# Halves of tokens for the second layer's input, and its first two score blocks inside the first gate projection

## The chip, the cores and the metric

The kernel runs on one core of one Trainium2 chip. The metric is the device time of one execution in microseconds; less is better. The kernel uses five engines: TensorE (PE; its weight loads are listed as PEld), VectorE (DVE), ScalarE (ACT), GpSimd (POOL) and SyncE (SP), which here only issues DMAs.

## The reference

Two layers over 1024 tokens of width 1024, and a final norm. Layer 0 is a gated delta rule with 8 heads; layer 1 is causal stick-breaking attention with 8 heads of 128.

```python
def stick_breaking_branch(h, w_in, w_out):
    q, k, v, gate = jnp.split(h @ w_in, 4, axis=-1)      # 8 heads of 128 each
    ...
        z = jnp.einsum('bhqd,bhsd->bhqs', q_blk, k).astype(jnp.float32) * scale
        log_1m = jnp.where(mask, jax.nn.log_sigmoid(-z), 0.0)
        tail = lax.cumsum(log_1m, axis=3, reverse=True) - log_1m
        A = jnp.where(mask, jnp.exp(jax.nn.log_sigmoid(z) + tail), 0.0)
        return jnp.einsum('bhqs,bhsd->bhqd', A.astype(v.dtype), v)
    ...
    return (o * jax.nn.silu(gate)) @ w_out

def reference(...):
    h = h + gated_deltanet_branch(rmsnorm(h, norm_w[0]), ...)
    h = h + stick_breaking_branch(rmsnorm(h, norm_w[1]), ...)
    return rmsnorm(h, final_norm_w)
```

## The kernel before

**Layout.** The residual `xT` is kept with its 1024 channels on the partitions, as eight blocks `cb` of 128 channels by 1024 tokens (five in `home`, three in `late`). A projection of one block of 128 outputs is 48 matmuls over 512 tokens: 8 blocks of channels, two halves of tokens, and three parts, because each float32 product is made as w_hi·u_hi + w_hi·u_lo + w_lo·u_hi. The weights are split by ScalarE (`split_hi`, w_hi) and GpSimd (`split_lo`, w_lo). The input is split by ScalarE (`u_upper`: u_hi = xT times the norm weight, rounded) and VectorE (`u_lower`: u_lo, what is left of it). The norm's factor per token is applied later, to the products.

**Groups and banks.** Every 24 matmuls over one half of the tokens form a group. Groups are numbered through the whole kernel and take PSUM banks 0 and 1 in turn; `proj_ready` counts those that TensorE has finished, `proj_taken` those that ScalarE or VectorE has read. TensorE starts a group only when the one two before it has been taken. `("b", h, b)` is a projection of head h in the second layer: b = 0 is q, 1 is k, 2 the gate, 3 is v.

**End of the first layer.** The output projection's last 16 groups (`last_group`, 6 matmuls each) run as i = 0 to 15, with half = i // 8 and cb = i % 8: first all blocks for the first 512 tokens, then all for the second. VectorE adds each group to `xT` (`add_output`, line 1197). After the add of a second-half group, ScalarE does `u_upper(1, cb)` over all 1024 tokens (line 789) and `square(1, cb)` (line 783), GpSimd adds the squares (`add_squares`, line 637), VectorE does `u_lower(1, cb)` over all 1024 tokens (line 1079), and only then its next add. square(cb) waits for the sum two blocks back. ScalarE's and GpSimd's streams also hold the splits of the first weights of layer 1 there, before block 4 and at the end.

**Start of the second layer.** TensorE runs ("b", 0, 0) block by block as u_lo comes, with `block_sum(1)` (line 1517: the sum of the squares over the channels) after 36 of its 48 matmuls, then ("b", 0, 1), then `rms_to_tokens(1)` (line 1525), then the gate ("b", 0, 2) and v ("b", 0, 3). ScalarE makes the norm's factor out of block_sum (lines 794, 796) and then takes each group (`take_b`, line 806). Then come a meeting of all engines (`all_arrived(…, 2)`), needed because the attention's buffers lie where others lay, and the scores.

**Attention.** Each head has eight blocks of queries, longest first. For a block, TensorE makes the scores into banks 2 and 3 or 4 and 5 (`scores`, line 1739), VectorE masks the diagonal (`mask`, line 1409), ScalarE takes Abs, Exp and Ln (`softplus`, lines 1020 to 1024), VectorE adds (`softplus_sum`, 1414), scans (`scan`, 1421) and subtracts (`exponent`, 1428, counted by `arg_done`), and ScalarE takes Exp (1031). `scores(h, s + 2)` waits for the exponent of block s, whose banks it takes. Between these, `attend` gives TensorE the matmuls of the next head's four projections, in numbers written out by hand (`STEP_FILL`). On VectorE q and k are scaled by `scale_qk` (lines 1395 and 1397, counted by `bqk_done`). For head 0 VectorE's stream is scale_qk, mask(0, 0), softplus_sum(0, 0), mask(0, 1), scan(0, 0), exponent(0, 0), and then `attend`, which begins with softplus_sum(0, 1), mask(0, 2), scan(0, 1).

Every engine runs its instructions in the order written; a wait holds up all that stands behind it on that engine. The end of the kernel is the output projection and the final norm.

Of the kernel before, what the change touches and what calls it, by code (L numbers as in the profile page):

```python
# [22 lines left out]
ALU = mybir.AluOpType  # L23
ACT = mybir.ActivationFunctionType
F32 = mybir.dt.float32
# [5 lines left out]
KB = D // P  # L31
NC = T // P
H = 8
HALF = 512
MMS = 3 * KB
# [46 lines left out]
def build(nc, x, norm_w, a_w_in, a_conv_w, a_a_log, a_dt_bias, a_o_norm, a_w_out,  # L82
          b_w_in, b_w_out, final_norm_w, out):
    V, A, G, PE = nc.vector, nc.scalar, nc.gpsimd, nc.tensor
# [10 lines left out]
    with ExitStack() as ctx:  # L95
# [8 lines left out]
        u_hi = sb("u_hi", [P, KB, T], F32R)  # L104
# [3 lines left out]
        u_lo = sb("u_lo", [P, KB, T], F32R)  # L108
# [8 lines left out]
        cols = sb("cols", [P, P])  # L117
# [4 lines left out]
        NORM_COL, ONORM_COL = 96, 120  # L122
# [5 lines left out]
        def xT(cb):  # L128

            return home[:, cb, :] if cb < HOME else late[:, cb - HOME, :]  # L130
# [102 lines left out]
        proj_ready, proj_taken = sem("proj_ready"), sem("proj_taken")  # L233
        u_hi_done, u_lo_done = sem("u_hi_done"), sem("u_lo_done")
# [11 lines left out]
        rst_ready, rst_done = sem("rst_ready"), sem("rst_done")  # L246
# [96 lines left out]
        FIRST, FREED = {}, {}  # L343
# [6 lines left out]
        LAST_GROUP = FIRST["last", 0]  # L350
# [37 lines left out]
        U_ROUND = {"gate": 0, ("b", 0, 0): 1, ("out", 0): 2}  # L388
        BY_K = ("gate", ("z", H - 1), ("early", 0), ("b", 0, 0), ("out", 0))

        def products(key, first, last):

            n, by_k, ks = NUMBER[key], key in BY_K, heads_of(key)
            for m in range(first, last):
                if by_k:
                    k, half, part = m // 6, m % 6 // 3, m % 3
                else:
                    half, k, part = m // (3 * ks), m % (3 * ks) // 3, m % 3
                if m == 0:
                    PE.wait_ge(lo_done, n + 1)  # L400
                if k == 0 and part == 0 and n > 0:

                    PE.wait_ge(proj_taken, FIRST[key] + half - 1)
                if key in U_ROUND and half == 0 and part == 0:
                    PE.wait_ge(u_lo_done, KB * U_ROUND[key] + k + 1)
                if key == ("early", 0) and half == 0 and part == 0:
                    PE.wait_ge(oe_lo, k + 1)
                mm = PE.matmul(psum[:, half], (w_hi, w_hi, w_lo)[part][:, n % 2, k],  # L408
                               (u_hi, u_lo, u_hi)[part][:, k, half * HALF:(half + 1) * HALF],
                               start=k == 0 and part == 0, stop=k == ks - 1 and part == 2)  # L410
                if k == ks - 1 and part == 2:
                    mm.then_inc(proj_ready, 1)
                elif key == ("z", H - 1) and half == 1 and part == 2:
                    mm.then_inc(u_free, 1)
# [62 lines left out]
        def half_range(half):  # L477

            return slice(half * HALF, (half + 1) * HALF)
# [299 lines left out]
        def _(act):  # L779
            def square(rnd, cb):  # L780
                if cb >= 3:
                    acc_done.wait(act, rnd, cb - 2)
                A.activation(acc[:, :] if cb == 0 else sq[:, cb % 2], xT(cb), ACT.Square
                             ).then_inc(sq_done.handle, 1)

            def u_upper(rnd, cb):

                col = NORM_COL + KB * rnd + cb
                A.activation(u_hi[:, cb, :], xT(cb), ACT.Copy, scale=cols[:, col:col + 1]
                             ).then_inc(u_hi_done, 1)  # L790
# [194 lines left out]
            norm_scale(H - 1, 1)  # L985
            late_hi(H - 1, 1)

            for cb in range(KB):
                if cb == KB // 2:
                    split_hi(("b", 0, 0))  # L990
                act.wait_ge(proj_taken, LAST_GROUP + KB + cb + 1)
                if cb == EARLY:
                    act.wait_ge(proj_ready, FREED["last", 1])
                u_upper(1, cb)
                square(1, cb)
            split_hi(("b", 0, 1))
            inverse_rms(1)
            arrive(act)
# [12 lines left out]
                if half == 1:  # L1011
                    split_hi(after_next(("b", nh, b)))

            for e in range(7):
                take_b(0, e)

            def softplus(h, s):
                w, slot, bk = (Q_BLOCKS[s] + 1) * P, s % 2, 2 + 2 * (s % 2)
                mask_done.wait(act, h, s + 1)
                A.activation(soft[:, slot, 0:w], banks(bk)[:, 0:w], ACT.Abs).then_inc(soft_a.handle, 1)  # L1020
                soft_a.wait(act, h, s + 1)
                A.activation(soft[:, slot, 0:w], soft[:, slot, 0:w], ACT.Exp, scale=-1.0).then_inc(soft_b.handle, 1)
                soft_b.wait(act, h, s + 1)
                A.activation(soft[:, slot, 0:w], soft[:, slot, 0:w], ACT.Ln, bias=1.0).then_inc(soft_c.handle, 1)
# [21 lines left out]
                    fill.to(STEP_AT[4 * s + 2])  # L1046
                fill.to(QUAD - MMS)

            for s in range(2):
                softplus(0, s)  # L1050
            for h in range(H - 1):
                attend(h, True)
            attend(H - 1, False)
# [21 lines left out]
        def _(dve):  # L1075
            def u_lower(rnd, cb):
                col = NORM_COL + KB * rnd + cb
                dve.wait_ge(u_hi_done, KB * rnd + cb + 1)
                V.scalar_tensor_tensor(out=u_lo[:, cb, :], in0=xT(cb), scalar=cols[:, col:col + 1],  # L1079
                                       in1=u_hi[:, cb, :].bitcast(F32), op0=ALU.mult, op1=ALU.subtract  # L1080
                                       ).then_inc(u_lo_done, 1)

            def output_lower(rnd, k):

                dve.wait_ge(u_hi_done, KB * rnd + k + 1)
                V.tensor_tensor(u_lo[:, k, :], o_all[:, k, :], u_hi[:, k, :].bitcast(F32),
                                ALU.subtract).then_inc(u_lo_done, 1)
# [30 lines left out]
            def by_head(t):  # L1118
# [18 lines left out]
                                   op0=ALU.max, op1=ALU.add).then_inc(gate_dve, 1)  # L1137
            dve.wait_ge(gate_dve, 4)
            V.scalar_tensor_tensor(out=graw[:, :, :], in0=by_head(gtmp[:, 3]), scalar=-1.0,
                                   in1=row_a[:, 2, :].unsqueeze(2).broadcast_to((P, H, NC)),  # L1140
                                   op0=ALU.mult, op1=ALU.mult).then_inc(gate_dve, 1)
# [6 lines left out]
                                   in0=gtmp[:, 0].rearrange("p n h -> p (n h)").rearrange("p (h n) -> p h n", h=H),  # L1148
                                   scalar=-1.0, in1=gates[:, :, 0, :],
                                   op0=ALU.mult, op1=ALU.mult).then_inc(gate_dve, 1)  # L1150
# [233 lines left out]
            late_lo(H - 1, 1, 4)  # L1384
            for i in range(2, 2 * KB):
                add_output(i % KB, LAST_GROUP + i, 16 * (KB - HOME))
                if i >= KB:
                    u_lower(1, i % KB)
            arrive(dve)
            rms_by_tokens(1)  # L1390
            all_arrived(dve, 2)
# [55 lines left out]
            def attend(h, follow):  # L1447
                for s in range(NC):
                    ahead = (h, s + 1) if s + 1 < NC else (h + 1, 0)
                    there = follow or s + 1 < NC  # L1450
                    if there:
                        softplus_sum(*ahead)
                    if s + 2 < NC:
                        mask(h, s + 2)
                    elif follow:
                        mask(h + 1, s + 2 - NC)
                    if there:
                        scan(*ahead)
                    copy_aT(h, s, 0)
                    if s == 0:  # L1460
                        scale_v(h, 0)
                    if there:
                        exponent(*ahead)
                    copy_aT(h, s, 1)
                    if s == 0:
                        scale_v(h, 1)
                    if s == 4:
                        gate_out(h, 0)
                    if s == 5 and follow:
                        scale_qk(h + 1)  # L1470
                    if not follow and s < H - 1:
                        output_lower(2, s)
                gate_out(h, 1)

            dve.sem_inc(bo_done.handle, 2)
# [18 lines left out]
                V.tensor_tensor(xT(cb)[:, half_range(half)], psum[:, half], xT(cb)[:, half_range(half)], ALU.add  # L1494
                                ).then_inc(proj_taken, 1)

            output_lower(2, H - 1)
            for cb in range(KB):
                for half in range(2):
                    add_block(cb, half)  # L1500
# [1 line left out]
            for n in range(NC):  # L1502
                dve.wait_ge(fin_rs, n + 1)
                if n >= 4:
                    dve.wait_ge(out_done[n % 4], 16 * (n // 4))
                V.scalar_tensor_tensor(out=fin_o[:, n % 4], in0=banks(FIN_BANKS[n % 4]), scalar=fin_s[:, n, 1:2],
                                       in1=fin_w[:, :], op0=ALU.mult, op1=ALU.mult).then_inc(fin_done, 1)
# [3 lines left out]
        def _(pe):  # L1511
# [210 lines left out]
            products(("b", 0, 0), 36, 2 * MMS)  # L1722
            products(("b", 0, 1), 0, 2 * MMS)
            rms_to_tokens(1)
            for b in range(2, 4):
                products(("b", 0, b), 0, 2 * MMS)

            def project(h, first, last):

# [5 lines left out]
            def scores(h, s):  # L1735
                w, bk, qb = (Q_BLOCKS[s] + 1) * P, 2 + 2 * (s % 2), Q_BLOCKS[s]
                for c in range(0, w, HALF):
                    n = min(HALF, w - c)
                    mm = PE.matmul(psum[:, bk + c // HALF, 0:n], b_q[:, qb * P:(qb + 1) * P],  # L1739
                                   b_k[:, c:c + n], start=True, stop=True)  # L1740
                mm.then_inc(sc_ready.handle, 1)
# [67 lines left out]

            all_arrived(pe, 2)  # L1810
            bqk_done.wait(pe, 0, 2)
            for s in range(2):
                scores(0, s)
            for h in range(H - 1):
                attend(h, True)
            attend(H - 1, False)
# [36 lines left out]
```

## Time and profile before

| | us |
|---|---|
| Median of 3 runs (1483.81 to 1485.61) | 1483.94 |
| The profiled execution | 1485.75 |
| Its span in the trace | 1484.0 |
| TensorE matmul busy | 1389.5 (94%) |
| VectorE busy | 894.7 (60%) |
| ScalarE busy | 638.0 (43%) |
| GpSimd busy | 433.8 (29%) |

The profile is one execution. Times in the rows are microseconds from the start of its span, and 1.75 us of the profiled execution lie around the span. The busy share of TensorE counts pipelined matmuls and is no measure of its speed; its clock is given as the share of full speed that was granted, 1.00 for 2.4 GHz and 0.50 for 1.2 GHz. In a timeline, a bracket holds how long the engine was idle ahead of the row and which operation ended that.

### The profile page before, as it was taken

The numbers are of one execution on the slowest core, as the hardware profiler recorded it, in microseconds if no ns is written. First come the engines' busy times: TensorE is split into PE (matmuls) and PEld (weight loads), VectorE is DVE, ScalarE is ACT, GpSimd is POOL, SyncE is SP. The second block draws the span as 40 slices with busy tenths as digits, with TensorE's granted clock in tenths as the row PEclk, the third lists the DMA queues.
The fourth block names the chain that finished last, engine by engine and source line by source line (L and its number), as shares of the span: only waits on it lengthen the run. The fifth ranks groups of instructions, "written<-read, shape, count | busy, mean of one in ns | idle before, by whom it ended". The sixth has DMA issues, their size and how long they took to land.

```text
span 1484.0 us, 18475 instructions
## 1 busy us (share of the span) xinstructions
PE 1389.5 (94%) x7351; PEld 1137.4 (77%) x7351; DVE 894.7 (60%) x1532; ACT 638.0 (43%) x879; POOL 433.8 (29%) x230
## 2 busy tenths in 40 slices
PE   5898999999999999988996989999999999998897
PEld 4687787888888888877884768778787877876785
DVE  7387777869697878776336145564546455557313
ACT  6153435253535353542325235544454445546113
POOL 6443334334233333434125311221122122211120
PEclk9999999999999999998999989999999999999999
DMA  7211110101111111030211200111111111000302
GB/s 188 55 29 29 29 36 22 51 22 37 36 36 29 36 36 36 23 120 12 75 43 57 57 29 29 29 44 29 29 29 43 29 29 29 29 30 0 114 29 114
DMA packets 97190, 65.20 MB, mean 44 GB/s; under 512 B 2401, under 2 KB 91602, under 8 KB 97106
## 3 DMA queue, kind: packets, MB, share of 16 engines
q1 hardware_dynamic: 97106, 64.04, 14.5%
q8 instruction: 58, 0.95, 0.3%
q14 instruction: 26, 0.21, 0.0%
HBM read 53.54 MB, written 10.49 MB: 43 GB/s over the span
## 4 chain that ended last, share of the span: by engine, by line
PE 80%; DVE 12%; ACT 3%; issue 2%; POOL 1%; DMA 0%; POOLq 0%; SPq 0%; DVEq 0%; PEldq 0%; ACTq 0%
PE psum L408 51%; PE psum L1739 4%; PE psum L1765 4%; DVE terms L1299 3%; PE psum L1752 2%; PE psum L1681 2%; PE psum L1626 2%; PE psum L1696 2%; PE psum L1651 2%; PE psum L1672 2%; DVE stick L1421 1%; PE psum L1635 1%; DVE small_L L1284 1%; PE psum L1577 1%; DVE Xs L1292 1%
## 5 line engine op out<-in xcount | busy, mean ns | idle before, releaser
L408 PE MATMUL psum<-u_hi,w_hi 128*128 128x512 f32 x1264 | 523.9, 414 | 27.7 <-DVE u_lo L1079 7.6
L408 PE MATMUL psum<-u_lo,w_hi 128*128 128x512 f32 x1264 | 517.5, 409 | 0.0
L408 PE MATMUL psum<-u_hi,w_lo 128*128 128x512 f32 x1264 | 506.8, 401 | 0.0
L381 POOL TENSOR_TENSOR w_lo<-w_raw,w_hi 128x1024 fp32r<-128x1024 f32 (+1 forms) x83 | 211.9, 2554 | 716.8 <-ACT w_hi L376 716.8
L408 PEld LDWEIGHTS psum<-u_hi,w_hi 128*128 128x128 f32 x1264 | 240.8, 190 | 82.8 <-issue 21.7
L408 PEld LDWEIGHTS psum<-u_lo,w_hi 128*128 128x128 f32 x1264 | 240.8, 190 | 50.5 <-issue 7.2
L408 PEld LDWEIGHTS psum<-u_hi,w_lo 128*128 128x128 f32 x1264 | 240.4, 190 | 49.7 <-issue 3.8
L376 ACT ACTIVATE w_hi<-w_raw 128x1024 fp32r<-128x1024 f32 (+1 forms) x83 | 85.8, 1034 | 159.0 <-PE psum L408 114.3
L708 POOL TENSOR_TENSOR Lb<-dec,level 128x512 f32<-128x512 f32 (+1 forms) x64 | 89.0, 1406 | 126.2 <-PE psum L1681 68.9
L1168 DVE SCALAR_TENSOR_TENSOR late<-raw,cols,late 128x1024 f32<-128x1024 f32 x72 | 120.1, 1668 | 1.9
L1020 ACT ACTIVATE soft<-psum 128x1024 f32<-128x1024 f32 (+3 forms) x64 | 41.7, 652 | 162.1 <-DVE psum L1409 161.5
L1409 DVE TENSOR_TENSOR psum<-psum,causal 128x128 f32<-128x128 f32 x64 | 19.0, 297 | 143.7 <-PE psum L1739 143.7
L915 ACT ACTIVATE v_new<-psum 128x128 f32<-128x128 f32 x64 | 17.7, 277 | 188.5 <-PE psum L1597 188.5
L1421 DVE TENSOR_TENSOR_SCAN stick<-soft 128x1024 f32<-128x1024 f32 (+3 forms) x64 | 97.7, 1526 | 0.0
L1436 DVE COPY aT<-psum 128x512 f32<-128x512 f32 (+1 forms) x96 | 52.3, 545 | 69.3 <-PE psum L1752 69.3
L1739 PE MATMUL psum<-b_k,b_q 128*128 128x512 f32 (+1 forms) x192 | 76.4, 509 | 15.3 <-DVE stick L1428 14.9
L1765 PEld LDWEIGHTS psum<-aT,b_v 128*128 128x128 f32 x576 | 75.0, 195 | 4.5
L1189 DVE TENSOR_TENSOR raw<-psum,rsb 128x512 f32<-128x512 f32 x64 | 43.8, 687 | 56.5 <-PE psum L408 56.5
L1299 DVE TENSOR_TENSOR terms<-Xs,small_T 128x16 f32<-128x16 f32 (+14 forms) x120 | 71.5, 596 | 9.7 <-DVE small_T L1304 0.5
L806 ACT ACTIVATE b_raw<-psum 128x512 f32<-128x512 f32 x64 | 38.0, 593 | 91.2 <-PE psum L408 91.1
L1765 PE MATMUL psum<-aT,b_v 128*128 128x128 f32 x576 | 76.0, 278 | 0.0
L1739 PEld LDWEIGHTS psum<-b_k,b_q 128*128 128x128 f32 x192 | 35.7, 194 | 41.5 <-DVE stick L1428 17.9
(208 smaller groups left out, 2022.2 us busy)
## 6 DMA issues: line engine op xcount, KB each, us to landing
w_raw<-in_a_w_in SPq DMA_DIRECT2D x33, 512.0 KB, 4.1
w_raw<-in_b_w_in SPq DMA_DIRECT2D x32, 512.0 KB, 4.0
x_stage<-in_x SPq DMA_DIRECT2D x8, 512.0 KB, 7.4
w_raw<-in_b_w_out SPq DMA_DIRECT2D x8, 512.0 KB, 3.6
out<-fin_o SPq DMA_DIRECT2D x8, 512.0 KB, 2.6
resid<-late SPq DMA_DIRECT2D x6, 512.0 KB, 2.6
o_rows<-o_nrm SPq DMA_DIRECT2D x12, 256.0 KB, 2.0
w_raw<-in_a_w_out SPq DMA_DIRECT2D x8, 384.0 KB, 3.2
```

The costliest lines, as they stand in the source:

```text
L376: A.activation(tiles(w_hi, key), tiles(w_raw, key), ACT.Copy).then_inc(hi_done, 1)
L381: G.tensor_tensor(tiles(w_lo, key), tiles(w_raw, key), tiles(w_hi, key).bitcast(F32), ALU.subtract).then_inc(lo_done, 1)
L408: mm = PE.matmul(psum[:, half], (w_hi, w_hi, w_lo)[part][:, n % 2, k], (u_hi, u_lo, u_hi)[part][:, k, half * HALF:(half + 1) * HALF], star ...
L708: G.tensor_tensor(Lb[:, g, :, used], half_of(dec, g)[:, :, used], level[:, l:l + 1, used].broadcast_to((P, 4, used.stop)), ALU.mult).then_ ...
L1020: A.activation(soft[:, slot, 0:w], banks(bk)[:, 0:w], ACT.Abs).then_inc(soft_a.handle, 1)
L1168: V.scalar_tensor_tensor(out=conv[:, s], in0=tap, scalar=by, in1=conv[:, s], op0=ALU.mult, op1=ALU.add).then_inc(convs.handle, 1)
L1189: V.tensor_tensor(raw[:, slot, 3 + half * HALF:3 + (half + 1) * HALF], psum[:, half], rsb[:, half_range(half)], ALU.mult).then_inc(proj_ta ...
L1299: V.tensor_tensor(terms[:, :, 0:r + 1], row_L[:, r % 2, :, 0:r + 1], small_T[:, :, 0:r + 1], ALU.mult).then_inc(terms_done.handle, 1)
L1421: V.tensor_tensor_scan(stick[:, slot, 0:w][:, ::-1], soft[:, slot, 0:w][:, ::-1], soft[:, slot, 0:w][:, ::-1], 0.0, ALU.add, ALU.bypass).t ...
L1436: V.tensor_copy(aT[:, s % 2, 4 * g:4 * g + n], bank(6, n)).then_inc(at_done.handle, 1)
L1739: mm = PE.matmul(psum[:, bk + c // HALF, 0:n], b_q[:, qb * P:(qb + 1) * P], b_k[:, c:c + n], start=True, stop=True)
L1765: mm = PE.matmul(psum[:, 7, t], b_v[:, blk, :], aT[:, s % 2, blk], start=blk == 0, stop=blk == qb)
```

## The change

The input of the second layer is made in halves of 512 tokens: the first halves of u_hi and u_lo of a block follow its first-half group, the second halves its second-half group. VectorE does each half of u_lo one add later than its block's own add (in the first sweep two adds later). The squares stay whole. As there are now sixteen counts of u_lo_done for this layer, the later waits count from 3·KB.

In TensorE's stream, the meeting of the engines, the wait for q and k, and scores(0, 0) move to the middle of the gate's projection, and scores(0, 1) to its end, ahead of v's projection. ScalarE's stream is changed to match: softplus(0, 0) ahead of the take of the gate's second half, softplus(0, 1) ahead of that of v's first half. VectorE's stream of the attention stays as it was.

```diff
@@ products
-                    PE.wait_ge(u_lo_done, KB * U_ROUND[key] + k + 1)
+                    PE.wait_ge(u_lo_done, (0, 2 * KB, 3 * KB)[U_ROUND[key]] + k + 1)
@@ scalar
+            def u_upper_half(cb, half):
+
+                col = NORM_COL + KB + cb
+                A.activation(u_hi[:, cb, half_range(half)], xT(cb)[:, half_range(half)], ACT.Copy,
+                             scale=cols[:, col:col + 1]).then_inc(u_hi_done, 1)
...
-            for cb in range(KB):
-                if cb == KB // 2:
+            for i in range(2 * KB):
+                half, cb = i // KB, i % KB
+                if i == KB + KB // 2:
                     split_hi(("b", 0, 0))
-                act.wait_ge(proj_taken, LAST_GROUP + KB + cb + 1)
+                act.wait_ge(proj_taken, LAST_GROUP + i + 1)
                 if cb == EARLY:
-                    act.wait_ge(proj_ready, FREED["last", 1])
-                u_upper(1, cb)
-                square(1, cb)
+                    act.wait_ge(proj_ready, LAST_GROUP + KB * (half + 1))
+                u_upper_half(cb, half)
+                if half == 1:
+                    square(1, cb)
             split_hi(("b", 0, 1))
...
-            for e in range(7):
+            for e in range(5):
                 take_b(0, e)
...
-            for s in range(2):
-                softplus(0, s)
+            softplus(0, 0)
+            take_b(0, 5)
+            softplus(0, 1)
+            take_b(0, 6)
             for h in range(H - 1):
                 attend(h, True)
@@ vector
+            def u_lower_half(cb, half):
+                col = NORM_COL + KB + cb
+                dve.wait_ge(u_hi_done, KB + half * KB + cb + 1)
+                V.scalar_tensor_tensor(out=u_lo[:, cb, half_range(half)], in0=xT(cb)[:, half_range(half)],
+                                       scalar=cols[:, col:col + 1], in1=u_hi[:, cb, half_range(half)].bitcast(F32),
+                                       op0=ALU.mult, op1=ALU.subtract).then_inc(u_lo_done, 1)
...
             for i in range(2, 2 * KB):
                 add_output(i % KB, LAST_GROUP + i, 16 * (KB - HOME))
-                if i >= KB:
-                    u_lower(1, i % KB)
+                if i < KB:
+                    u_lower_half(i - 2, 0)
+                elif i == KB:
+                    for cb in range(KB - 2, KB):
+                        u_lower_half(cb, 0)
+                if i > KB:
+                    u_lower_half(i % KB - 1, 1)
+            u_lower_half(KB - 1, 1)
             arrive(dve)
...
-                        output_lower(2, s)
+                        output_lower(3, s)
...
-            output_lower(2, H - 1)
+            output_lower(3, H - 1)
@@ tensor
             rms_to_tokens(1)
-            for b in range(2, 4):
-                products(("b", 0, b), 0, 2 * MMS)
+            products(("b", 0, 2), 0, MMS)
...
             all_arrived(pe, 2)
             bqk_done.wait(pe, 0, 2)
-            for s in range(2):
-                scores(0, s)
+            scores(0, 0)
+            products(("b", 0, 2), MMS, 2 * MMS)
+            pe.wait_ge(rst_done, 2)
+            scores(0, 1)
+            products(("b", 0, 3), 0, 2 * MMS)
```

## Rows read from the trace of the kernel before

**Rows 1.** The page: the chain's shares by engine, and a DMA issue.

```profile
PE 80%; DVE 12%; ACT 3%; issue 2%; POOL 1%; DMA 0%; POOLq 0%; SPq 0%; DVEq 0%; PEldq 0%; ACTq 0%
w_raw<-in_b_w_in SPq DMA_DIRECT2D x32, 512.0 KB, 4.0
```

**Rows 2.** The chain that ended last, 770 to 885: start, us, what.

```profile
782.50 7.06 PE psum L425 x30
...
805.81 0.69 DVE late L1197
...
809.14 0.69 DVE late L1197
...
813.18 9.16 PE psum L408 x33
...
827.32 11.17 PE psum L408 x48
...
840.17 21.88 PE psum L408 x96
...
864.13 1.03 ACT soft L1020
...
866.28 1.06 ACT soft L1024
```

**Rows 3.** Windows: stretch, us, busy time (count) of five engines, granted clock, DMA.

```profile
790.00:806.00 16.00, 8.78 (x34) 5.73 (x33) 9.89 (x11) 11.44 (x11) 9.30 (x4) 1.00 0.01 1
...
813.18:815.91 2.73, 2.73 (x6) 2.16 (x7) 1.49 (x1) 2.26 (x3) 2.59 (x2) 0.50 0.48 192
813.18:822.18 9.00, 9.00 (x33) 7.33 (x34) 1.49 (x1) 3.15 (x3) 8.71 (x4) 0.84 0.36 117
...
872.30:878.24 5.94, 5.94 (x17) 4.20 (x18) 3.92 (x3) 4.96 (x6) 2.37 (x1) 0.56 0.01 3
```

**Rows 4.** Timeline of GpSimd: start, us, line, operation, output and inputs, shapes, [idle before].

```profile
795.58 2.54 POOL L637 TENSOR_TENSOR acc<-acc,sq 128x1024 f32<-128x1024 f32 x1 [17.21 <-ACT sq L783]
...
802.02 2.78 POOL L637 TENSOR_TENSOR acc<-acc,sq 128x1024 f32<-128x1024 f32 x1 [0.55 <-ACT sq L783]
804.77 3.37 POOL L381 TENSOR_TENSOR w_lo<-w_raw,w_hi 128x1024 fp32r<-128x1024 f32 x1
808.09 12.54 POOL L637 TENSOR_TENSOR acc<-acc,sq 128x1024 f32<-128x1024 f32 x4
```

**Rows 5.** Timeline of VectorE, 770 to 885.

```profile
781.10 0.69 DVE L1208 TENSOR_TENSOR u_lo<-o_raw,u_hi 128x512 fp32r<-128x512 f32 x1 [0.70 <-ACT u_hi L904]
...
804.38 1.51 DVE L1079 SCALAR_TENSOR_TENSOR u_lo<-home,cols,u_hi 128x1024 fp32r<-128x1024 f32 x1 [1.22 <-ACT u_hi L789]
...
840.43 3.19 DVE L1395 SCALAR_TENSOR_TENSOR b_q<-b_raw,rsb 128x1024 f32<-128x1024 f32 x1
843.55 1.21 DVE L1397 TENSOR_TENSOR b_k<-b_raw,rsb 128x1024 f32<-128x1024 f32 x1
```

**Rows 6.** Timeline of ScalarE, 770 to 885.

```profile
780.44 0.63 ACT L904 ACTIVATE u_hi<-o_raw 128x512 fp32r<-128x512 f32 x1 [3.31 <-DVE o_raw L1232]
...
791.36 1.04 ACT L783 ACTIVATE acc<-home 128x1024 f32<-128x1024 f32 x1
...
825.25 1.06 ACT L796 ACTIVATE rsb<-rsb 128x1024 f32<-128x1024 f32 x1
```

**Rows 7.** Timeline of TensorE, line 1739; the last row is of the chain.

```profile
861.88 3.38 PE L1739 MATMUL psum<-b_k,b_q 128*128 128x512 f32 x8
872.30 2.93 PE L1739 MATMUL psum<-b_k,b_q 128*128 128x512 f32 x4 [7.03 <-DVE stick L1428]
...
924.28 1.99 PE L1739 MATMUL psum<-b_k,b_q 128*128 128x512 f32 x4
...
941.36 1.45 PE L1739 MATMUL psum<-b_k,b_q 128*128 128x512 f32 x4
...
990.74 2.00 PE psum L1739 x4
```

## The prediction, made before the change was run

> **What bounds the kernel now.** I read the page first. TensorE is busy nearly all the time, and the chain that ended last lies on it for 80% of the span [rows 1]: a gain must be time in which TensorE stands still or runs slowly. So I followed that chain only from 770 to 885 us, where the second layer's input is made and its attention begins [rows 2].
>
> Two holes stand there. In the first the chain goes round "add on VectorE, u_hi on ScalarE, u_lo on VectorE, next add" with a period of 3.34 us (the adds at 805.81 and 809.14): u_upper and u_lower handle 1024 tokens behind each second-half group, and the next add is queued behind them, so TensorE starts a group of 1.41 us (30 matmuls in 7.06) only every 3.34 us. The product ("b", 0, 0) runs freely only from 813.18. In the second, TensorE computes both score blocks at 861.88, then waits 7.03 us until `exponent(0, 0)` lets it take the third at 872.30 [rows 2, 7]. Behind each hole the granted clock is at its lower level, 1.2 GHz: 0.50 for 2.73 us after the first, 0.56 for 5.94 us after the second [rows 3].
>
> **Second part of the change: the score blocks.** Times are those of before, as if nothing ahead had moved.
>
> Step 1, TensorE. From 840.17 it runs 96 matmuls in 21.88 us, 0.228 each [rows 2]. Now it takes 24 of them (to 845.6), scores(0, 0), 24 (to 852.8), scores(0, 1) (to 854.4), 48. Scores cost 3.38 us for both [rows 7], so all ends at 865.3, as before. I cost the two extra changes of operation at nothing.
>
> Step 2, the added waits. `all_arrived` now stands in front of 72 matmuls. Its last arrivals are ScalarE, after `inverse_rms` (826.3), and GpSimd, after a w_lo that follows the last sum (820.6, and 2.4 more) [rows 4, 6]; covered by 19 us. `bqk_done` needs b_k, at 843.55+1.21 = 844.76 [rows 5]: covered by 0.8 us. The wait for rst_done is older still.
>
> Step 3, VectorE. Its mask(0, 0) falls at 847.4. ScalarE takes the gate's first half (now at 845.8), then Abs, Exp, Ln of softplus(0, 0), three instructions from 864.13 to 867.3 in the rows, 3.2 us [rows 2], done at 850.9. mask(0, 1) then stands in VectorE's queue in front of scan(0, 0), waiting for scores(0, 1) at 854.4; behind it wait scan, exponent and softplus_sum(0, 1). scan meets GpSimd's next w_lo, which starts first at about 854.4, and I let it wait for its end (as b_q did, below): scan until 859.1, exponent until 860.3. TensorE asks for this at 865.3, so 5 us are spare.
>
> Step 4, ScalarE. The take of the gate's second half is queued behind softplus(0, 0), whose end at 850.9 lies ahead of the 852.8 at which that half is ready. v's second half in bank 1 needs it by 859.9. Behind it w_hi of the next head's q is made at 854.3 instead of 852.7, its w_lo at 856.7, needed at 866.8. softplus(0, 1) ends at 857.6, ahead of v's first half at 859.9. The DMA of the weights two ahead starts up to 4 us later and lands in 4.0 [rows 1], long ahead of its use.
>
> Step 5, what is gained. The wait of 7.03 us goes. The slow clock goes too: from the third block of head 0 to the first of head 1 it is 924.28-872.30 = 51.98 us, one head later 990.74-941.36 = 49.38 [rows 7]; 2.60 us. Together **9.6 us**. What is late next is nothing on TensorE; later heads have the same queues as before.
>
> **First part: halves.** Step 6, what is removed and added. Eight u_hi and eight u_lo of 1024 tokens become sixteen of 512. A half costs 0.63 us on ScalarE and 0.69 on VectorE, starting 0.6 apart [rows 5, 6]. The eight halves in the first sweep cost nothing: one add and one half take VectorE 1.3 us against TensorE's 1.41 per group, and ScalarE and GpSimd idle there. The last two run behind add 8, so add 9 starts at 791.5.
>
> Step 7, what else paces the second sweep. GpSimd adds the squares, and ScalarE's square(cb) waits for that sum two blocks back. From 802.02 GpSimd never pauses until 820.59 [rows 4]: it is next behind the cycle of Step 6. The profile shows how it mixes with VectorE. w_lo starts at 804.77 while u_lo (from 804.38) had waited for the sum that ends at 804.80; u_lo ends at 805.89, 1.09 later, and w_lo 2.25 after that, 3.37 in all [rows 4, 5]. The sum of 2.54 us has 0.3 of such waiting. So these two kinds, both reading two operands from SBUF, exclude one another, 2.3 us pure on GpSimd and 0.55 for a half on VectorE; the adds, which read PSUM, are not held (0.68 at 809.14, beside a sum). This speaks against the halves: a u_lo that meets a sum holds the adds behind it for up to 2.3 us. The Trainium skill has it as a rule (SBUF — State Buffer, "SBUF: two separate sides": VectorE with two SBUF inputs and GpSimd take one port pair in turn, and the later one waits for the whole instruction of the other). By that rule the sums end as in Step 8; if the two only slowed each other by chance of these rows, they would end 3.5 us sooner.
>
> Step 8, GpSimd under that exclusion, from rows. square(1) needs add 9: add 792.15, u_hi half 792.8, square 793.8 (1.04) [rows 6]; the first sum starts at 793.9 instead of 795.58. Then seven sums and one w_lo of 2.3 us, with the six halves of 0.55 to 0.6 that still come between them: 18.4+3.5, end at **815.8** instead of 820.6. On the way w_lo of ("b", 0, 0) is ready at 804.8 and the last add at 806.0; ScalarE's squares are ready each time.
>
> Step 9, TensorE. The product begins at 804.9, passes to its second bank at 806.05, and then needs the 9.00 us that its 33 matmuls took behind the hole of before, 1.5 of it slow clock [rows 3]: 815.05. `block_sum` has to wait for GpSimd until 815.8; before it began at 822.18. From there on all is as before: Ln, Exp, take, next product 5.14 us later [rows 2]. Gain **6.3 us**. What binds next is GpSimd, and 0.8 us behind it TensorE itself.
>
> SP's three stores of `resid` wait for adds 13 to 15, now at 800 to 806; they took 6.96 us in all and block nobody sooner. The two-input count of u_lo_done and the 3 in output_lower are bookkeeping.
>
> **Sum.** 9.6+6.3 = 15.9 us, all in TensorE's standing still or slow. The profiled execution took 1485.75 us (span 1484.0, 1.75 around it), so it would take 1469.85; the median of the runs lies 1.8 lower, at 1483.94, which gives **1468.0**.
>
> **Bounds.** Second part: if b_q and b_k both meet a GpSimd operation (b_q took 3.19 us where b_k of the same size took 1.21 [rows 5]: one does already), b_k comes 2.0 later, TensorE waits 1.2, gain 8.4; 9.6 is the top, since no pause and no slow clock is then left to gain. First part: low end, GpSimd's chain keeps its length of before, 25.0 us from 795.58 to 820.6: end at 818.9, gain 3.3. High end, no exclusion, 812.3 by the sums and 812 by TensorE: gain 9.8. I take 6.3, since the row at 804.77 splits to the hundredth into its two parts.
>
> **Rivals.** (a) The halves hardly help, because GpSimd's chain is as long as before and only starts 1.7 us sooner: 3.3+9.6 = 12.9, 1471.0. For it: it is the gapless engine. Against: part of its length is u_lo of 1024 tokens standing in its way, which is now 512. (b) No real exclusion among shorter operations: 9.8+9.6 = 19.4, 1464.5. (c) b_k late, or a clock that stays low longer after 801.8 (the group of add 13 ends there and TensorE idles 3 us): 1.2 to 3 us lost, 1469.2 to 1471. (d) Slower. The clock: TensorE works in bursts from 790 on, now with gaps up to 3 us, and if it stayed at 1.2 GHz through ("b", 0, 0) and ("b", 0, 1), every us of it would cost 0.5. It loses everything from 32 us of low clock on; 40 us give 1488. Against it: 5.94 us is what followed a pause of 7, and the bursts of 790 to 806 were granted 1.00 [rows 3]. (e) The change does not do what it says: the wait for `exponent(0, 0)` reappears in front of scores(0, 2) and the sums end as before: 1484. It would need over 5 us more on VectorE in Step 3, and Step 7 to be wrong as well.
>
> **How the numbers follow.** Forecast 1466 to 1469.5: 0.55. (a) 0.15, (b) 0.09, (c) 0.12, (d) 0.04, (e) 0.05. From 1464.5 (b) to 1473 (a and c together) leaves some 0.15 out. A measurement of this kernel tells a change of some 0.2%, 3 us, from none. Faster by more: 0.91; within: 0.05; slower by more: 0.04.
>
> **What would show it.** Right: half-size u_lo between adds from 782 on; the sums on GpSimd gapless from about 794 to 816; `block_sum` near 815.8; scores(0, 0) 5.4 us after the rms product without a wait; scores(0, 2) directly behind v's last product at full clock; heads of 66.5 us. Wrong: a wait on b_k before scores(0, 0) (Step 2), on stick before scores(0, 2) (Steps 3, 4), `block_sum` at 818 or later (Step 8) or sooner than 814 (Step 7), low clock behind 806 for more than 3 us (Step 9).

## The result and the profile after

| | before | changed |
|---|---|---|
| Median, us | 1485.11 (1483.81 to 1485.61, 5 runs) | 1469.0 (1467.34 to 1469.86, 5 runs) |
| Profiled execution, us | 1485.75 | 1469.78 |
| Its span, us | 1484.0 | 1468.1 |

The ratio is 0.9891, with an interval of 0.9881 to 0.9902: 16 us faster, 1.1%. The forecast was 15.9 us and a median of 1468.0. The median of the kernel before, which had been 1483.94, was 1485.11 in these five runs, so the forecast's median was taken from a number 1.2 us too low, and the measured one lies 1.0 above it.

The chain by engine, which answers to [rows 1], from the page of the changed kernel:

```profile
PE 80%; DVE 12%; POOL 3%; ACT 2%; issue 2%; DMA 0%; POOLq 0%; SPq 0%; DVEq 0%; PEldq 0%; ACTq 0%
```

GpSimd's share rose from 1% to 3% and ScalarE's fell from 3% to 2%. The same chain in order of time (start, us, what), to be read beside [rows 2], shows where it went:

```profile
794.66 2.41 POOL acc L637
797.21 2.66 POOL acc L637
800.01 2.65 POOL acc L637
802.71 2.67 issue
805.38 2.83 POOL acc L637
...
813.97 2.39 POOL acc L637
816.41 1.98 PE psum L1540 x4
...
834.53 5.56 PE psum L408 x24
840.09 1.72 PE psum L1761 x4
841.80 5.49 PE psum L408 x24
847.29 1.50 PE psum L1761 x4
848.80 10.93 PE psum L408 x48
859.73 1.29 PE psum L1761 x4
```

The round of add, u_hi and u_lo is gone from it. In its place stand GpSimd's seven sums (the 2.67 us of "issue" are its w_lo of ("b", 0, 0)), with at most 0.14 us between two, from 794.66 to block_sum. Behind the rms product TensorE then goes through the gate, the two score blocks and v to the third block at 859.6 with nothing between.

TensorE's timeline beside [rows 7]; a bracket would be a wait:

```profile
805.47 0.50 PE L408 MATMUL psum<-u_hi,w_hi 128*128 128x512 f32 x1 [2.75 <-POOL w_lo L381]
806.62 0.79 PE L408 MATMUL psum<-u_hi,w_hi 128*128 128x512 f32 x1 [0.19 <-DVE late L1214]
816.41 1.98 PE L1540 MATMUL psum<-acc,ones 128*128 128x512 f32 x4 [0.42 <-POOL acc L637]
...
859.57 1.45 PE L1761 MATMUL psum<-b_k,b_q 128*128 128x512 f32 x4
...
908.94 1.98 PE L1761 MATMUL psum<-b_k,b_q 128*128 128x512 f32 x4
```

The window of 5.94 us from the third block on, in the form of [rows 3], has a granted clock of 1.00, where before it had 0.56:

```profile
859.57:865.51 5.94, 5.94 (x30) 4.66 (x29) 4.40 (x5) 4.07 (x6) 4.11 (x1) 1.00 0.01 3
```

**The bill**, from the two traces. The changed one enters this stage 0.42 us later (at the first group of the output projection that follows a pause of TensorE of 1.43 us, here called the first stalled group, which starts at 782.92 instead of 782.50): -0.42. From there to block_sum it takes 33.49 us instead of 39.68: +6.19. From block_sum to the gate's first matmul the two differ by 0.13: -0.13. From that matmul to the third score block it takes 25.04 instead of 32.13: +7.09. From the third block to the next head's first it takes 49.37 instead of 51.98: +2.61. The rest of the kernel gave +0.56. The sum is 15.90, the difference of the spans.

### The profile page after: what moved, and what is told of

It is laid out like the page before. It is cut to its first block, busy times and chain, and to the rows that moved or that the text cites. A ratio compares the mean times of both kernels' runs of the same rounds, so it can differ in the third digit from the quotient of the medians.

```text
span 1468.1 us, 18492 instructions
## 1 busy us (share of the span) xinstructions
PE 1386.8 (94%) x7351; PEld 1135.2 (77%) x7351; DVE 903.0 (62%) x1540; ACT 640.1 (44%) x887; POOL 435.1 (30%) x230
## 4 chain that ended last, share of the span: by engine, by line
PE 80%; DVE 12%; POOL 3%; ACT 2%; issue 2%; DMA 0%; POOLq 0%; SPq 0%; DVEq 0%; PEldq 0%; ACTq 0%
PE psum L408 51%; PE psum L1761 4%; PE psum L1787 4%; DVE terms L1316 3%; POOL acc L637 2%; PE psum L1774 2%; PE psum L1704 2%; PE psum L1649 2%; PE psum L1719 2%; PE psum L1674 2%; PE psum L1695 2%; PE psum L1658 1%; DVE small_L L1301 1%; DVE stick L1444 1%; PE psum L1600 1%
```

## The experiments

All ratios are to the kernel before, in runs on the same chip. A span is that of one profiled execution, and those of one kernel differ by up to 4 us; the stretches between two marks of a trace, which repeat more closely, are the better measure.

**1 and 2. Each part alone.** `scores_only` is the kernel before with the second part, `halves_only` the changed kernel without it.

```diff
 scores_only, against before
-            for b in range(2, 4):
-                products(("b", 0, b), 0, 2 * MMS)
+            products(("b", 0, 2), 0, MMS)
...
-            for s in range(2):
-                scores(0, s)
+            scores(0, 0)
+            products(("b", 0, 2), MMS, 2 * MMS)
+            pe.wait_ge(rst_done, 2)
+            scores(0, 1)
+            products(("b", 0, 3), 0, 2 * MMS)
 (and ScalarE's stream as in the change)
```

> The kernel before with the second part of the change alone (score blocks of head 0 inside and behind the gate's projection, ScalarE's stream to match); u_hi and u_lo stay whole. Theory: this part is worth the wait of 7.03 us and 2.60 us of slow clock, whatever the first part does. 9.6 us less than before, span about 1474.4. scores(0, 0) starts without a wait near 845.6, block_sum stays at 822.2. Rival (the parts share a gain, for instance because the clock or the queues behind depend on both): 6 us or less here.

Measured: median 1476.26, ratio 0.9932 (0.9917 to 0.9948), some 10 us faster; span 1474.6, 9.4 less.

> The changed kernel with the score blocks put back behind v's projection: the halves alone. Theory: block_sum begins 6.2 us earlier than before, and the wait on exponent(0, 0) of 7.0 us with its slow clock stays. 6.2 us less than before, span about 1477.8; together with the other part alone 15.8. Rival: TensorE's earlier start is lost in the wait behind the scores, because that wait hangs on ScalarE or VectorE and not on TensorE: 0 to 3 us.

Measured: median 1479.86, ratio 0.9953 (0.9938 to 0.9969), some 7 us faster; span 1478.0, 6.0 less. Its timeline of TensorE keeps the whole second hole, moved forward:

```profile
816.33 1.98 PE L1538 MATMUL psum<-acc,ones 128*128 128x512 f32 x4 [0.49 <-POOL acc L637]
...
856.15 3.38 PE L1760 MATMUL psum<-b_k,b_q 128*128 128x512 f32 x8
866.56 2.93 PE L1760 MATMUL psum<-b_k,b_q 128*128 128x512 f32 x4 [7.03 <-DVE stick L1449]
...
918.24 1.98 PE L1760 MATMUL psum<-b_k,b_q 128*128 128x512 f32 x4
```

The wait is 7.03 us as before, and the stretch behind it 918.24-866.56 = 51.68 (51.98 before). The spans add up: 9.4+6.0 = 15.4 against 15.9 for both. The stretches of the bill do so more closely. In `scores_only` it takes 82.70 us from the first stalled group to the third block instead of 89.80, and 49.38 from there to the next head instead of 51.98: 9.7. In `halves_only` it takes 33.48 us from the first stalled group to block_sum instead of 39.68: 6.2. Together that is 15.9, and both at once gave 6.19+7.09+2.61, also 15.9. The rivals (a shared gain, or the first gain lost in the second wait) are out. The halving and the delay of each u_lo by one add were not run apart.

**3. Is the 2.6 us behind the hole the clock?** `keep_clock` gives TensorE useless work in the hole.

```diff
             for s in range(2):
                 scores(0, s)
+            for _ in range(7):
+                PE.matmul(psum[:, 6], b_q[:, 0:P], b_k[:, 0:HALF], start=True, stop=True)
```

> The kernel before with seven extra matmuls of b_k and b_q over 512 columns (two records of 0.42 us each) in TensorE's pause behind scores(0, 1), into a bank that nobody reads; nothing else is changed. They fill some 6.0 of the 7.03 us. Theory: the excess of head 0, 51.98 against 49.38 us, is the low clock behind the pause. With TensorE kept busy the clock stays at its upper level and the kernel is 2.6 us faster, though it does more. Rival: the excess is head 0 catching up in its queues (softplus, scan, w_lo): no change, 0 us.

```profile
867.06 6.17 PE L1815 MATMUL psum<-b_k,b_q 128*128 128x512 f32 x14
874.26 1.56 PE L1739 MATMUL psum<-b_k,b_q 128*128 128x512 f32 x4 [1.02 <-DVE stick L1428]
...
923.74 1.98 PE L1739 MATMUL psum<-b_k,b_q 128*128 128x512 f32 x4
```

The third block takes 1.56 us instead of 2.93, the granted clock of the 5.94 us from it on is 1.00 instead of 0.56, and the stretch to the next head is 49.48 instead of 51.98. Median 1483.01, ratio 0.9978 (0.9967 to 0.9989): 1.6 to 4.9 us faster with more work in it. (The profiled execution itself is only 0.4 us shorter than that of the kernel before: it comes to the first stalled group 1.2 us later and loses 0.8 in low clock behind the first hole, where the code is the same. The stretch carries this reading.) So the 9.6 us of the second part are 7.0 of standing still and 2.6 of low clock, and the second goes with the first.

**4. Why two blocks move and not one.** `first_only` leaves scores(0, 1) behind v.

```diff
-            pe.wait_ge(rst_done, 2)
-            scores(0, 1)
             products(("b", 0, 3), 0, 2 * MMS)
+            pe.wait_ge(rst_done, 2)
+            scores(0, 1)
...
             take_b(0, 5)
-            softplus(0, 1)
             take_b(0, 6)
+            softplus(0, 1)
```

> The changed kernel with scores(0, 1) behind v's projection instead of behind the gate's, and softplus(0, 1) behind the take of v's first half. Theory: on VectorE scan(0, 0) stands behind mask(0, 1), so exponent(0, 0) ends only some 3.9 us (mask 0.3, scan 2.3, exponent 1.2) behind these scores and TensorE waits that long in front of scores(0, 2), with up to 2 us of low clock behind it: 3.9 to 6 us slower than the changed kernel, span 1472 to 1474. Rival: it is enough that scores(0, 0) is early: the same as the changed kernel within 0.5 us.

The chain of this kernel, and the last row as its timeline has it, with the wait:

```profile
857.65 1.52 PE psum L1761 x4
859.16 0.02 issue
859.19 0.30 DVE psum L1432
859.49 2.20 DVE stick L1444
861.69 0.02 issue
861.71 1.24 DVE stick L1451
862.95 0.04 issue
862.99 2.23 PE psum L1761 x4
```

```profile
862.99 2.23 PE L1761 MATMUL psum<-b_k,b_q 128*128 128x512 f32 x4 [3.84 <-DVE stick L1451]
```

TensorE waits 3.84 us, and the stretch to the next head's first block takes 914.06-862.99 = 51.07 instead of 49.37, 1.7 more, with a granted clock of 0.71 in its first 5.9 us. Span 1474.0, 5.9 more than the changed kernel; ratio to before 0.9926 (0.991 to 0.9942). Against `halves_only` (span 1478.0) the early scores(0, 0) is worth 4.0 us alone, not 9.9, as long as scan(0, 0) stands in VectorE's queue behind a mask that needs scores(0, 1).

**5. Do u_lo and the sums exclude one another?** In `no_lock` the second halves of u_lo take one operand from PSUM. That bank does not hold the residual, so this kernel leaves out the right u_lo for half of the tokens; only its times are of use. It was run beside the changed kernel (`changed_again`).

```diff
-                V.scalar_tensor_tensor(out=u_lo[:, cb, half_range(half)], in0=xT(cb)[:, half_range(half)],
+                V.scalar_tensor_tensor(out=u_lo[:, cb, half_range(half)],
+                                       in0=psum[:, 7] if half == 1 else xT(cb)[:, half_range(half)],
```

> The changed kernel as it is, once more, as the yardstick of the three kernels run beside it: 15 to 17 us less than before.

> The changed kernel, but the second halves of u_lo read a PSUM bank instead of the residual (so the second layer gets a wrong u_lo for half of its tokens; the sizes and the order stay). Theory: it is having both operands in SBUF that makes u_lo and GpSimd's sums take turns. Then these u_lo take some 0.75 us instead of 2.3 beside the sums, the adds keep TensorE's pace, the seven sums and one w_lo take 2.35 us each without a break and end at about 813.5 instead of 816.4; TensorE reaches block_sum at about 814.4. 2 to 2.5 us faster than the changed kernel. Rival: GpSimd and VectorE slow one another whatever they read (its sums are long by themselves): nothing changes, u_lo stay at 2.3 us.

VectorE in the changed kernel (first profiled execution), the first row while GpSimd is idle, and in `no_lock`:

```profile
782.73 0.74 DVE L1096 SCALAR_TENSOR_TENSOR u_lo<-home,cols,u_hi 128x512 fp32r<-128x512 f32 x1
...
795.32 2.30 DVE L1096 SCALAR_TENSOR_TENSOR u_lo<-home,cols,u_hi 128x512 fp32r<-128x512 f32 x1
797.54 0.68 DVE L1214 TENSOR_TENSOR home<-psum,home 128x512 f32<-128x512 f32 x1
798.14 2.27 DVE L1096 SCALAR_TENSOR_TENSOR u_lo<-home,cols,u_hi 128x512 fp32r<-128x512 f32 x1
```

```profile
795.63 0.75 DVE L1096 SCALAR_TENSOR_TENSOR u_lo<-psum,cols,u_hi 128x512 fp32r<-128x512 f32 x1
796.29 0.68 DVE L1215 TENSOR_TENSOR late<-psum,late 128x512 f32<-128x512 f32 x1
```

GpSimd in the two, in the same order:

```profile
802.63 2.79 POOL L381 TENSOR_TENSOR w_lo<-w_raw,w_hi 128x1024 fp32r<-128x1024 f32 x1
805.38 10.97 POOL L637 TENSOR_TENSOR acc<-acc,sq 128x1024 f32<-128x1024 f32 x4
```

```profile
800.92 2.36 POOL L381 TENSOR_TENSOR w_lo<-w_raw,w_hi 128x1024 fp32r<-128x1024 f32 x1
803.23 9.97 POOL L637 TENSOR_TENSOR acc<-acc,sq 128x1024 f32<-128x1024 f32 x4
```

Beside a sum, the same instruction of the same size takes 0.75 us with an operand in PSUM and 2.3 with both in SBUF. Both in SBUF and GpSimd idle, it takes 0.74 (782.73): PSUM is no faster by itself. GpSimd's w_lo comes down from 2.79 to 2.36, its last four sums from 10.97 to 9.97. This is the exclusion that the rows at 804.38 and 804.77 had shown, now with the operand as the only thing changed. `changed_again` had 1468.73, ratio 0.9888 (0.9873 to 0.9903); `no_lock` 1467.56, 0.9881 (0.9866 to 0.9895): 1.2 us in the medians instead of the 2 to 2.5 expected, and the intervals overlap, so the gain is read from the trace. Counted from the first stalled group, the sums end 2.0 us sooner, but the product behind block_sum starts only 1.3 us sooner (37.45 instead of 38.76). TensorE took the rest back: it pauses 4.45 us for w_lo instead of 2.75, its next 36 matmuls run at a granted clock of 0.76 instead of 0.84, and it then no longer waits for the sums at all. Two engines arrive at block_sum nearly together, so speeding up one gives only what the other leaves.

**6. What binds the first part now?** `adds_first` lets the adds go ahead of the u_lo that would hold them up, and splits the weights of ("b", 0, 0) one block earlier.

```diff
-                if i > KB:
-                    u_lower_half(i % KB - 1, 1)
-            u_lower_half(KB - 1, 1)
+                if i in (KB + 1, KB + 2, KB + 4, KB + 6):
+                    u_lower_half({1: 0, 2: 1, 4: 2, 6: 3}[i - KB], 1)
+            for cb in range(4, KB):
+                u_lower_half(cb, 1)
 (and split_hi and split_lo of ("b", 0, 0) one block earlier)
```

> The changed kernel with VectorE's second halves of u_lo moved behind the adds where these would be held up (u_lo 2 behind add 12, 3 behind add 14, 4 to 7 behind add 15), and the split of the weights of (b, 0, 0) one block earlier on ScalarE and GpSimd. Theory: TensorE gets (b, 0, 0) about 2.8 us sooner, near 802.7, but block_sum still has to wait for GpSimd's last sum at about 816.4. The wait of 0.4 us in front of block_sum grows to some 3 us, and the kernel is at most 0.5 us faster than the changed one. Rival: what binds is the start of (b, 0, 0), behind the adds and w_lo: 2.5 us faster.

```profile
801.75 0.51 PE L408 MATMUL psum<-u_hi,w_hi 128*128 128x512 f32 x1 [2.66 <-POOL w_lo L381]
815.42 3.78 PE L1541 MATMUL psum<-acc,ones 128*128 128x512 f32 x4 [5.17 <-POOL acc L637]
```

TensorE starts 2.8 us sooner, as said (19.79 instead of 22.55 us behind the first stalled group), and block_sum starts when it did (33.46 and 33.49): the last sum is the bound, not the start of the product. But the expectation that this costs nothing failed. The wait grew to 5.17 us, not 3, because the 36 matmuls ahead of it now ran at full clock (8.5 us, where the changed kernel took 10.52), and behind that wait the low clock stood where it hurts: block_sum took 3.78 us instead of 1.98, and from its start to the rms product it was 18.65 us instead of 16.28. Median 1471.02, ratio 0.9905 (0.989 to 0.9919), 2.3 us slower than `changed_again`.

**7. The sums off the path.** `late_sum` is `adds_first` with block_sum half a projection later, and with ScalarE free to take q before it makes the factor.

```diff
-            products(("b", 0, 0), 0, 36)
+            products(("b", 0, 0), 0, 2 * MMS)
+            products(("b", 0, 1), 0, MMS)
             block_sum(1)
             arrive(pe)
-            products(("b", 0, 0), 36, 2 * MMS)
-            products(("b", 0, 1), 0, 2 * MMS)
+            products(("b", 0, 1), MMS, 2 * MMS)
...
+                if i == KB + 6:
+                    split_hi(("b", 0, 1))
...
-            split_hi(("b", 0, 1))
-            inverse_rms(1)
-            arrive(act)
-            all_arrived(act, 2)
...
-            for e in range(5):
+            act.wait_ge(res_out, 32 * (KB - HOME))
+            act.wait_ge(u_lo_done, 3 * KB)
+            for e in range(2):
+                take_b(0, e)
+            inverse_rms(1)
+            arrive(act)
+            all_arrived(act, 2)
+            for e in range(2, 5):
                 take_b(0, e)
...
+                if cb == 6:
+                    split_lo(("b", 0, 1))
                 add_squares(1, cb)
-            split_lo(("b", 0, 1))
```

> adds_first, and block_sum taken off TensorE's way: it stands in the middle of (b, 0, 1), the weights of (b, 0, 1) are split ahead of the sixth sum, and ScalarE takes both halves of (b, 0, 0) ahead of the norm's factor, waiting only for the stores and the u_lo whose buffers it writes over. Theory: with GpSimd's sums off the path TensorE runs from (b, 0, 0) at about 802.7 through q and k without a wait and is some 4.5 us ahead at the product that carries the factor to the tokens: span about 1463.5, 4 to 5 us faster than the changed kernel and 20 faster than before. Rival: the factor, the meeting of the engines or the scaling of q and k then come last and give the wait back in front of scores(0, 0): 0 to 2 us faster than the changed kernel.

```profile
800.36 0.68 PE L408 MATMUL psum<-u_hi,w_hi 128*128 128x512 f32 x1 [2.66 <-POOL w_lo L381]
813.33 0.47 PE L408 MATMUL psum<-u_hi,w_hi 128*128 128x512 f32 x1 [0.18 <-ACT b_raw L813]
818.88 1.88 PE L1548 MATMUL psum<-acc,ones 128*128 128x512 f32 x4
826.43 1.84 PE L1556 MATMUL psum<-ident,rsb 128*128 128x1 f32 x16
```

No wait for the sums is left, and nothing else took its place. The rms product stands 45.85 us behind the first stalled group, 3.9 sooner than in the changed kernel (49.77). Median 1465.48, ratio 0.9866 (0.9848 to 0.9883), and 3.3 us below `changed_again`, less than the 4 to 5 expected. The later block_sum, the earlier weights of ("b", 0, 1) and ScalarE's new order came together; what each gives was not run. On another chip (`late_sum_again`) it had 1464.98, ratio 0.9856 (0.984 to 0.9873).

> The same as late_sum, as the yardstick of the kernel run beside it: 19 to 20 us less than before.

**8. The clock behind the pause that is left.** `late_sum_warm` is `late_sum` with this pause of 2.7 us filled.

```diff
+            for _ in range(3):
+                PE.matmul(psum[:, 6], ones[:, :], home[:, 0, 0:HALF], start=True, stop=True)
             products(("b", 0, 0), 0, 2 * MMS)
```

> late_sum with three extra matmuls (two records of 0.42 us each, into a bank that nobody reads) in TensorE's pause of 2.7 us ahead of (b, 0, 0), while it waits for w_lo. Theory: the 1.9 us by which the 48 matmuls behind that pause took longer (12.8 against 10.9) are low clock that the pause brings about; with it filled the kernel is up to 1.9 us faster than late_sum. Rival: the clock of that stretch falls or not by something else (in adds_first it stayed at 1.00 behind the same pause): no change, within 0.5 us.

The window of its first 48 matmuls (it opens 0.3 us ahead of the first) and the one of `late_sum`, each with the granted clock in the third place from the end:

```profile
800.60:812.25 11.65, 11.37 (x49) 8.96 (x49) 6.84 (x4) 6.10 (x8) 11.36 (x6) 1.00 0.23 74
```

```profile
800.36:813.33 12.97, 12.79 (x49) 10.14 (x49) 6.51 (x4) 6.10 (x8) 12.68 (x5) 0.87 0.21 63
```

In the stretch the theory holds: clock 1.00, and the second projection starts 31.14 us behind the first stalled group instead of 32.75 (32.74 in `late_sum_again`). In the time it does not show: median 1465.61, ratio 0.9862 (0.9847 to 0.9877), beside 0.9856 for the kernel without it. Whether 1.6 us are there to be had stays open. The profiled execution lost as much again in its last stage: from the rms product to the end it took 1.5 us more than `late_sum`, and from 1320 to 1375 its granted clock was 0.88, where both executions of `late_sum` had 0.91.

**9. The thin margin.** `scores_sooner` asks for b_k 8 matmuls earlier than the changed kernel.

```diff
-            products(("b", 0, 2), 0, MMS)
+            products(("b", 0, 2), 0, 16)
...
             scores(0, 0)
-            products(("b", 0, 2), MMS, 2 * MMS)
+            products(("b", 0, 2), 16, 2 * MMS)
```

> The changed kernel with scores(0, 0) 8 matmuls (1.8 us) further ahead in the gate's first half: behind 16 of its matmuls instead of 24. Theory: b_k is ready only some 0.8 us before the changed kernel asks for it, so here TensorE waits about 1.0 us for it in front of scores(0, 0) and everything behind comes 1.0 us later than in the changed kernel. Rival: the margin is larger than the forecast's 0.8 us, or the wait is made up by the 5 us that are spare further on: no change in the time.

```profile
838.21 1.95 PE L1761 MATMUL psum<-b_k,b_q 128*128 128x512 f32 x4 [1.00 <-DVE b_k L1420]
```

The wait is 1.00 us, ended by b_k: 8 matmuls of 0.228 are 1.82, so the margin was 0.8. Ratio 0.99 (0.9885 to 0.9914) against 0.9891 and 0.9888 for the changed kernel; the ratio alone does not tell 1 us from none, and the changed kernel was not run beside this one. The stretch does: from block_sum to the third block it is 44.36 us instead of 43.16 (43.13 in `changed_again`), so the wait is not made up. The 5 us that are spare further on do not give it back, as they are VectorE's and not TensorE's.

## Why the prediction was right

The mechanism was the one named in both parts, and no term of the sum was off by more than 0.6 us. That the total hit 15.9 to the tenth is partly luck: terms that the forecast did not have (-0.42 ahead of the stage, +0.56 behind it, -0.13 between) cancel, and small errors of Steps 6 to 9 do so among themselves.

**Steps 1, 2 and 5** came out to a tenth. The wait of 7.03 us is gone and so are 2.61 us of low clock (forecast 2.60). b_k was ready 0.81 us ahead of its use (forecast 0.8), and experiment 9 turned that margin into a wait of 1.00. Experiment 3 shows that the clock is the cause of the 2.6 us, which the prediction had only read off two stretches.

**Steps 3 and 4.** The price of scan(0, 0) beside GpSimd was named: VectorE has

```profile
848.83 0.30 DVE L1432 TENSOR_TENSOR psum<-psum,causal 128x128 f32<-128x128 f32 x1 [2.19 <-PE psum L1761]
849.04 4.46 DVE L1444 TENSOR_TENSOR_SCAN stick<-soft 128x1024 f32<-128x1024 f32 x1
853.54 1.22 DVE L1451 TENSOR_TENSOR stick<-psum,stick 128x1024 f32<-128x1024 f32 x1
```

and exponent(0, 0) ends at 854.8, 4.8 us before TensorE asks for it at 859.6 (forecast 5). What the forecast left out is the other side: GpSimd's scaling of the gate, queued behind w_lo, stood behind this scan and took 4.40 us. Nobody waited for it.

**Step 6** was slightly too kind. A half of u_hi with its scale took 0.72 us on ScalarE, not the 0.63 of the row it was taken from, which has no scale. VectorE also fell behind TensorE's pace once in the first sweep: add 6 started at 787.75 after 0.36 us of idling for which the profile names no cause, and add 8 came at 790.27, 0.27 later than before when the 0.42 of the start is taken off. So the halves of the first sweep cost 0.3 us and not nothing, and the first sum started 0.3 later than forecast.

**Steps 7 and 8** carried the first part. The sums ended at 816.36, that is 815.9 with the 0.42 taken off (forecast 815.8): they started 0.3 later and took 21.7 us instead of 21.9. Experiment 5 shows the exclusion to be the mechanism. It also set the pace of the adds, 2.8 us each from 794.7 on, by holding every u_lo until a sum or w_lo had ended.

**Step 9**, again with the 0.42 taken off. The product started at 805.05 (804.9) and changed bank at 806.2 (806.05). Its 33 matmuls took 9.37 us and not the 9.00 of before, so TensorE reached block_sum at 815.6 instead of 815.05, and waited 0.42 us instead of 0.8. The low clock behind 806.62 lasted 3.15 us (0.50 until 809.77), where the forecast had taken the 2.73 of before; by its own list, more than 3 us was a sign of being wrong. It cost nothing only because GpSimd's sums ended later still. The gain was 6.2 us (6.3).

**The rivals.** (a), a GpSimd chain of its old length, is refuted: 21.7 us instead of 25.0. (b), no exclusion, is refuted by experiment 5; that experiment also shows that 9.8 us would not have been reached without it, as TensorE comes next. (c) did not happen, but experiment 9 shows that it stood 0.8 us away. Its other half, a clock that stays low longer, came in small: 0.4 us longer than before, behind which TensorE still had to wait for the sums. (d), low clock through both projections, did not happen: from 809.77 on the matmuls follow one another at 0.23 us, as at full clock. (e) is out by experiments 1 and 2.

## What to carry to other kernels

A stall of TensorE that ends on another engine's queue can be filled with TensorE's own later work, and its worth is the stall and the slow clock behind it (7.0 and 2.6 us here). Look into the other engine's stream for what stands ahead of the awaited instruction: moving one of the two score blocks gave 5.9 us less than moving both. When a round trip is cut in pieces, ask which chain is gapless beside it; here it was GpSimd's sums, and starting TensorE earlier (`adds_first`) lost 2.3 us, while the same with their consumer taken later (`late_sum`) gained 3.3 (both against `changed_again`), though two further edits came with it.

## What the runs showed of the hardware

Filling a pause of TensorE with matmuls whose result is thrown away made the kernel faster (`keep_clock`, ratio 0.9978, 0.9967 to 0.9989). A wait moved behind TensorE's busy stretch cost more than its length: in `adds_first` 5.17 us of waiting were followed by a block_sum of 3.78 us instead of 1.98.

The low clock behind one and the same pause is not the same in every execution. Behind the pause of 2.33 us ahead of the second bank of ("b", 0, 0), the stretch to the next projection took 14.14 us in the kernel before and 14.11 in `scores_only`, at a granted clock of 0.90, but 14.90 in `keep_clock`, at 0.85, though the three have the same code up to there. Kernels differ too: behind 2.66 us the granted clock of the next matmuls was 1.00 in `adds_first`, and 0.87 in `late_sum` and again in `late_sum_again`; no run shows why. The stage ahead of the change differs between executions as well: the first stalled group came at 780.58 in `late_sum` and at 782.71 in `late_sum_again`, the same kernel. A gain of 1 or 2 us in this kernel is therefore read from a stretch of the trace, counted from a mark in it, rather than from a median.
